# Reordering three places of a two-block network on one core: a sum of squares ahead of a late weight chunk, the convolution between two query chunks, a mixture's first gather under the last gate chunk

## The reference

```python
h = layer_norm(x, ln_in_g, ln_in_b)
for i in range(DEPTH_2):
    proj = h @ w_in[i] + b_in[i]                       # a, g (convolution), q, k, v
    conv_out = conformer_conv(a, g, conv_w[i], conv_b[i], conv_ln_g[i], conv_ln_b[i])
    attn_out = neighbourhood_attention(q, k, v, rpb[i])
    mix = jnp.concatenate([conv_out, attn_out], -1) @ w_out[i] + b_out[i]
    h = layer_norm(DEEPNORM_ALPHA * h + mix, ln1_g[i], ln1_b[i])
    f = swiglu(h, ...) if i % 2 == 0 else moe_swiglu(h, ...)   # 8 experts, top 2, width 3584
    e = jax.nn.sigmoid(h @ ple_gate_w[i] + ple_gate_b[i]) * (p[i] @ ple_w[i])
    h = layer_norm(DEEPNORM_ALPHA * h + f + e, ln2_g[i], ln2_b[i])
```

## Time and profile before

| | |
|---|---|
| median of 3 runs | 2154.37 us (2154.33 to 2155.86) |
| the profiled execution | 2156.51 us, its span 2154.8 us |
| PE busy | 2082.8 us, 97% |
| DVE, ACT, POOL busy | 1569.8, 1282.1, 151.7 us |
| PE's longest waits by line | L969 for DVE 12.4, L613 for the arena-to-arena transfers 10.3 in two |
| share of the chain that ended last | PE 83%, DVE 8%, issue 3%, ACT 2%, DMA 2% |
| HBM | 267 GB/s over the span |

### The profile page before, as it was taken

One profiled execution on the slowest core, in us unless ns is written; L12 is line 12 of the kernel. 1 busy time (PEld: TensorE's weight loads), 2 busy tenths in 40 slices (PEclk: granted clock), 3 DMA queues, 4 the chain that ended last, 5 costly groups with the idle time before them and its releaser, 6 DMA issues.

```text
span 2154.8 us, 29826 instructions
## 1 busy us (share of the span) xinstructions
PE 2082.8 (97%) x11243; PEld 1731.1 (80%) x11243; DVE 1569.8 (73%) x1365; ACT 1282.1 (59%) x1280; POOL 151.7 (7%) x125
## 2 busy tenths in 40 slices
PE   9999999997999999989899999999999999999997
PEld 8977897776788999877677888888888888888875
DVE  6866544576367556646888888888888888888897
ACT  6765443353364334443667777676777777686674
POOL 0041010001024000020130000000000000000100
PEclk9999999999999999999899999999999999999999
DMA  5532594224626555643699999999999999999994
GB/s 217 194 108 99 192 340 163 76 103 169 227 94 224 179 193 179 234 129 123 241 375 392 377 367 379 375 373 369 378 368 368 377 366 378 375 373 368 381 387 183
DMA packets 88530, 581.50 MB, mean 270 GB/s; under 512 B 9968, under 2 KB 14064, under 8 KB 22528
## 3 DMA queue, kind: packets, MB, share of 16 engines
q1 hardware_dynamic: 80336, 549.42, 67.7%
q0 software_dynamic: 7648, 29.89, 3.9%
q10 hardware_dynamic: 464, 1.04, 0.1%
HBM read 559.93 MB, written 15.73 MB: 267 GB/s over the span
## 4 chain that ended last, share of the span: by engine, by line
PE 83%; DVE 8%; issue 3%; ACT 2%; DMA 2%; SPq 1%; POOL 0%; DVEq 0%; POOLq 0%; ACTq 0%
PE bank L613 75%; DVE wrest L2550 3%; DVE wrest L1952 1%; PE bank L1342 1%; SPq L400 1%; DMA ring<-in_w_moe 1%; PE bank L926 1%; PE bank L818 1%; PE bank L1149 1%; PE bank L924 0%; PE bank L905 0%; DMA arena<-arena 0%; DVE bst L2266 0%; DVE h L2276 0%; DVE arena L2524 0%
## 5 line engine op out<-in xcount | busy, mean ns | idle before, releaser
L2550 DVE TENSOR_TENSOR wrest<-ring,whi 128x2048 fp32r<-128x2048 f32 x378 | 853.4, 2307 | 89.8 <-ACT whi L1860 89.5
L1860 ACT ACTIVATE whi<-ring 128x2048 fp32r<-128x2048 f32 x374 | 696.7, 1917 | 70.6 <-DMA ring<-in_w_moe 66.2
L613 PE MATMUL bank<-whi,xgT 128*128 128x512 f32 x1008 | 406.5, 403 | 8.4 <-DVE wrest L2550 6.0
L613 PE MATMUL bank<-wrest,xgT 128*128 128x512 f32 x1008 | 398.0, 395 | 0.0
L613 PE MATMUL bank<-whi,xgR 128*128 128x512 f32 x1008 | 395.1, 392 | 0.0
L613 PEld LDWEIGHTS bank<-whi,xgT 128*128 128x128 f32 x1008 | 190.6, 189 | 53.2 <-DVE wrest L2550 9.6
L613 PEld LDWEIGHTS bank<-whi,xgR 128*128 128x128 f32 x1008 | 190.5, 189 | 46.9
L613 PEld LDWEIGHTS bank<-wrest,xgT 128*128 128x128 f32 x1008 | 189.8, 188 | 39.2
L613 PE MATMUL bank<-whi,hidE 128*128 128x512 f32 x504 | 201.9, 401 | 4.7 <-DVE hidR L2555 4.0
L613 PE MATMUL bank<-wrest,hidE 128*128 128x512 f32 x504 | 198.1, 393 | 0.0
L613 PE MATMUL bank<-whi,hidR 128*128 128x512 f32 x504 | 196.7, 390 | 0.0
(11 more groups left out here) (469 smaller groups left out, 3774.7 us busy)
## 6 DMA issues: line engine op xcount, KB each, us to landing
ring<-in_w_moe SPq DMA_DIRECT2D x378, 1024.0 KB, 4.8
ring<-in_w_dense SPq DMA_DIRECT2D x135, 1024.0 KB, 4.8
row<-in_rows POOLq DMA_DIRECT2D x17, 512.0 KB, 5.5
xg_rows<-ncR POOLq DMA_DIRECT2D x12, 512.0 KB, 24.4
y_rows<-arena POOLq DMA_DIRECT2D x9, 512.0 KB, 6.5
arena<-xg_rows SPq DMA_DIRECT2D x9, 512.0 KB, 5.4
arena<-arena SPq DMA_DIRECT2D x32, 142.0 KB, 5.1
arena<-in_tbias POOLq DMA_DIRECT2D x2, 1536.0 KB, 9.8
```

The lines of the kernel that those rows point to most:

```text
L613: ins = pe.matmul(out_, lhsT, rhs, start=start, stop=stop, **more)
L1860: S["w_hi"].on(a.activation(whi[:, n % HI_SLOTS, :], ring[:, c % RING, :], ACT.Copy))
L2550: S["w_lo"].on(v.tensor_tensor(wrest[:, s, :], ring[:, s, :], whi[:, n % HI_SLOTS, :].bitcast(F32), ALU.subtract))
```

## The change

**Start of layer 0.** ScalarE squares tile 0 of the output product ahead of the rounding of projection chunk 2. VectorE takes the rests of the turned tokens ahead of that chunk's rest.

**Convolution.** The two chunks of the convolution's weights move one place back in the stream of weights, between the two query chunks (`CONV_AT` 9 to 10), so that f 12 and 13 come ahead of the convolution, in both layers. The mean stands between f 14 and f 15. ScalarE copies f 12 and 13 out, and rounds mix chunks 1 and 2, ahead of the convolution's result; mix chunk 0, whose rounded copy lies where `stk` was, comes third. VectorE follows in that order.

**Start of the mixture.** `rank` stands in the middle of gate chunk 2, and `gather_first` behind that chunk, ahead of gate chunk 3. On ScalarE and VectorE the first expert chunks' roundings and rests, the first tokens' split and the gate embedding, now by token tile, are spread over the router's steps. `prime` (counts that stand for a "round minus one" of the loop) comes ahead of them. The transposes of the place matrix, and the copy of their result, move behind the eighth list, to bank 5.

```diff
@@
 PROJ_CHUNKS, MIX_CHUNKS, GATE_CHUNKS, ROW_CHUNKS = 11, 4, 4, 4
-LAYER_CHUNKS, CONV_AT, MIX_AT, GATE_AT = 21, 9, 13, 17
+LAYER_CHUNKS, CONV_AT, MIX_AT, GATE_AT = 21, 10, 13, 17
 SHIFTS, TAP_STEPS = 4, 8
@@
     _names("proj", 0) + _names("pT", 0) + _names("proj", 1, 2) + early + _names("proj", 4, 5, 6, 7, 8, 9, 10)
-    + _names("mix", 0, 1, 2, 3) + _names("gate", 0, 1) + _names("h", 4, 5) + _names("gate", 2, 3) + _names("h", 6, 7)
+    + _names("mix", 1, 2, 0, 3) + _names("gate", 0, 1) + _names("h", 4, 5) + _names("gate", 2, 3) + _names("h", 6, 7)
     for early in (_names("h", 0, 1) + _names("proj", 3) + _names("h", 2, 3),
                   _names("proj", 3) + _names("h", 0, 1, 2, 3)))
-LO_ORDER = (_names("pT", 0) + _names("proj", *range(PROJ_CHUNKS)) + _names("mix", *range(MIX_CHUNKS))
+LO_ORDER = (_names("pT", 0) + _names("proj", *range(PROJ_CHUNKS)) + _names("mix", 1, 2, 0, 3)
             + _names("gate", *range(GATE_CHUNKS)))
@@
                 for i in range(2):
-                    if c == LAYER_FIRST[i] + CONV_AT + 3:
+                    if c == LAYER_FIRST[i] + CONV_AT + 2:
                         stack(i)
@@
 
-                def features(first, end):
+                def features(first, end, between=None):
                     for f in range(first, end):
@@
                             give(1)
+                        elif between:
+                            between()
 
-                features(0, 12)
+                features(0, 14)
                 pe.wait_ge(stk_in, 16 * 16 * (i + 1))
@@
                         give(1)
-                features(12, 14)
-                wait(pe, "conv_ready", 4 * (i + 1))
-                for f in range(4):
-                    mean = pe.matmul(ps[6][:, 0:SEQ], ones, cc[:, f, :], start=f == 0, stop=f == 3)
-                S["cv_ps"].on(mean)
-                features(14, 16)
+
+                def conv_mean():
+
+                    wait(pe, "conv_ready", 4 * (i + 1))
+                    for f in range(4):
+                        mean = pe.matmul(ps[6][:, 0:SEQ], ones, cc[:, f, :], start=f == 0, stop=f == 3)
+                    S["cv_ps"].on(mean)
+
+                features(14, 16, conv_mean)
                 wait(pe, "p_act", 12 * (i + 1))
@@
                 for c in range(ROW_CHUNKS):
-                    ins = half_rows(w[c], c, 1, *hT, half_banks[1])
+                    if i and c == 2:
+                        half_rows(w[c], c, 1, *hT, half_banks[1], (0,))
+                        rank()
+                        half_rows(w[c], c, 1, *hT, half_banks[1], (1,))
+                        gather_first()
+                    else:
+                        ins = half_rows(w[c], c, 1, *hT, half_banks[1])
                     if c == ROW_CHUNKS - 1:
@@
                         turn_logits()
-                    if i and c == 2:
-                        rank()
-                if i:
-                    gather_first()
 
@@
 
-            wait(pe, "places", 3)
-            wait(pe, "m_xgv", 2)
-            for t in range(2):
-                ins = pe.transpose(ps[3][:, t * P:(t + 1) * P], selg[:, t, :], ident)
-            S["place_ps"].on(ins)
             prime(pe, "m_w2", "m_tr")
@@
                 expert_list(i, False)
+            wait(pe, "places", 3)
+            wait(pe, "pg_in", 8)
+            for t in range(2):
+                ins = pe.transpose(ps[5][:, t * P:(t + 1) * P], selg[:, t, :], ident)
+            S["place_ps"].on(ins)
             expert_list(last_list, True)
@@
             copy_m(3)
-            round_proj(0, 2, WO_FIRST)
 
@@
                     square_post(0)
+                    round_proj(0, 2, WO_FIRST)
                     copy_h(0, 0)
@@
 
-                for m in range(6):
+                for m in range(7):
                     if m < 3:
@@
                         round_proj(i, 10, first + 7)
+                        wait(a, "p_dve", 4 * i + 4)
                     for f in (2 * m, 2 * m + 1):
@@
                             keys(f)
+                round_early(1, 9)
+                round_early(2, 10)
                 for f in range(4):
@@
                 round_early(0, CONV_AT + 2)
-                round_early(1, 9)
-                wait(a, "p_dve", 4 * i + 4)
-                keys(12)
-                keys(13)
-                round_early(2, CONV_AT + 3)
                 wait(a, "cn_done", 3 * i + 1)
@@
                         round_dense(FF_FIRST + m, fhi[:, m % FF_HI_SLOTS, :], 0, FF_FIRST - 2 + 2 * m)
-                    gate_embedding(0)
+                    gate_embedding(0, 0)
+                    gate_embedding(0, 1)
 
-            def gate_embedding(i):
+            def gate_embedding(i, j):
 
-                for q in range(4):
-                    j, n = divmod(q, 2)
+                for n in range(2):
                     c = slice(n * 512, (n + 1) * 512)
-                    wait(a, "pg_in", 4 * i + q + 1)
+                    wait(a, "pg_in", 4 * i + 2 * j + n + 1)
                     S["ple_act"].on(a.activation(fe[:, j, c], fe[:, j, c], ACT.Sigmoid))
@@
             layer(1)
-            wait(a, "r_top", 2)
-            S["r_e"].on(a.activation(g12[:, 1, :], g12[:, 0, :], ACT.Exp))
 
@@
             prime(a, "m_sl", "m_hT")
+            round_ahead(0)
+            round_ahead(1)
+            wait(a, "r_top", 2)
+            S["r_e"].on(a.activation(g12[:, 1, :], g12[:, 0, :], ACT.Exp))
+            round_ahead(2)
+            gate_embedding(1, 0)
+            round_gathered(0, 2)
+            round_ahead(3)
+            gate_embedding(1, 1)
             wait(a, "router_done", 1)
             last_list = a.value_load(plan_i[0:1, 1 + SECONDS:2 + SECONDS], min_val=N_EXP - 1, max_val=LISTS - 1)
-            round_gathered(0, 2)
-            for n in range(AHEAD):
-                round_ahead(n)
-            gate_embedding(1)
             def expert_list(i, last):
@@
             def between_post():
-                rest_proj(0, 2)
                 rest_tokens(0, 0)
+                rest_proj(0, 2)
 
@@
                 rest_proj(i, 10)
-                rest_early(0)
                 rest_early(1)
+                rest_early(2)
+                rest_early(0)
 
@@
                                                        ALU.mult, ALU.add))
-                rest_early(2)
                 v.wait_ge(tb_in, 16 * (i + 1))
@@
 
-                    bias_embedding(0)
+                    bias_embedding(0, 0)
+                    bias_embedding(0, 1)
 
-            def bias_embedding(i):
+            def bias_embedding(i, j):
 
                 pb = row_of("ple_b", i + 2)
-                for q in range(4):
-                    j, n = divmod(q, 2)
+                for n in range(2):
                     c = slice(n * 512, (n + 1) * 512)
@@
                     S["pg_in"].on(v.tensor_tensor(fe[:, j, c], ps[half_banks[j][n]][:, :], pb[:, c], ALU.add))
-                v.wait_ge(S["pg_in"].sem, 4 * (i + 1))
-                rows_used.on(v.memset(nmax[:, 3:4], 0.0))
+                if j:
+                    v.wait_ge(S["pg_in"].sem, 4 * (i + 1))
+                    rows_used.on(v.memset(nmax[:, 3:4], 0.0))
 
@@
 
+            def rest_chunk(i, n):
+
+                wait(v, "w_hi", i * E_CHUNKS + (MOE_ROUNDED + n + 1))
+                s = (N_DENSE + n) % RING
+                S["w_lo"].on(v.tensor_tensor(wrest[:, s, :], ring[:, s, :], whi[:, n % HI_SLOTS, :].bitcast(F32),
+                                             ALU.subtract))
+
+            prime(v, "m_hid", "m_hr")
+            rest_chunk(0, 0)
+            bias_embedding(1, 0)
             wait(v, "rl_ps", 1)
@@
             io8 = many(iota[:, 0:N_EXP], 2, 1)
+            rest_chunk(0, 1)
             wait(v, "rl_ps", 2)
@@
 
-            def rest_chunk(i, n):
-
-                wait(v, "w_hi", i * E_CHUNKS + (MOE_ROUNDED + n + 1))
-                s = (N_DENSE + n) % RING
-                S["w_lo"].on(v.tensor_tensor(wrest[:, s, :], ring[:, s, :], whi[:, n % HI_SLOTS, :].bitcast(F32),
-                                             ALU.subtract))
-
             def rest_hid(i, j):
@@
                                                 float(N_EXP - 1), None, ALU.min))
+            rest_chunk(0, 2)
+            rest_gathered(0, 2)
             wait(v, "r_e", 1)
@@
             S["places"].on(v.memset(limit[:, 1:2], 0.0))
-
+            bias_embedding(1, 1)
+            rest_chunk(0, 3)
 
@@
 
-            rest_gathered(0, 2)
-            for n in range(AHEAD):
-                rest_chunk(0, n)
-            wait(v, "place_ps", 2)
-            S["places"].on(v.tensor_copy(selT[:, :, :], ps[3][:, 0:2 * P].rearrange("p (j n) -> p j n", j=2)))
-            bias_embedding(1)
-            prime(v, "m_hid", "m_hr")
             def expert_list(i, last):
@@
                     rest_chunk(i, n)
+                    if last and n == AHEAD + 2:
+                        wait(v, "place_ps", 2)
```

(8 more changed lines are left out.)

## The result

The changed kernel takes **2118.73 us** (median of 4 runs, 2117.69 to 2120.41) against 2155.11 us before (4 runs, 2154.33 to 2156.62): ratio **0.9831**, 95% interval 0.9814 to 0.9848. I had predicted 2117, in a range of 2111 to 2129. The profiled execution took 2120.41 us with a span of 2118.7; the trace of before has 2154.8, so 36.1 us are to be found.

A forecast was written before the change was run, and what follows sets the result against it. TensorE, busy 97% of the span, was taken as the bound, with gains where it stands still or runs slowly. Terms 11.2 + 7.0 + 6.6 + 13.0 = 37.8 us off the 2154.37 median give 2116.6, stated as 2117, range 2111 to 2129.

The forecast's parts named there:

- Part 1: Start of layer 0: squares ahead of the late chunk's rounding bring the second transposes from 522.36 to 511.1, gaining 11.2 us.
- Part 2: Convolution between the query chunks fills the wait for shifted copies: gains 7.0 us in layer 0, 6.6 in layer 1.
- The wait for the query copies: Before the scores, behind the last query tile: TensorE waits 2 us instead of 1.04.
- Rival D: Convolution: shifted copies come later, TensorE stops again, cold; part 2 keeps about 3 of 13.6: 2128; chance 0.08.
- Part 3: Start of the mixture: step 1's transposes of the first list start at 1045.9 instead of 1058.90, gaining 13.0 us.
- a stall of 2.0 us stays, too short, I judge, to cost clock: Before chunk 5 of the first list: TensorE waits 2.0 us beside GpSimd's product, with no loss of clock.
- three places where I wanted a granted clock of 1.00: Sign of being right: full granted clock at layer 0's token transposes, the convolutions and the first expert chunks.
- ScalarE's table loads: Ahead of chunk 5's rest: 7.4 us including two loads of 1.28, with no room for the skill's drain.
- Rival B: First list: five more GpSimd steps by chunk 21 cost 2.1 us each, 10.5 more: 2128; chance 0.08.
- Rival C: First list: expert chunks' transfers set the pace, so part 3 is worth only 5.8 us: 2124; chance 0.08.
- E: Slower: TensorE's clock falls to 1.2 GHz and stays there in the first list; a whole list gives 2234; chance 0.02.
- F: Nothing moves, because what is waited for is not what is named: 2154; chance 0.02.

The follow-up runs named there:

- p2_only: The kernel before with only the convolution moved between the query chunks, squares and mixture as before: 2142.29 us, ratio 0.9938.
- p1_only: The kernel before with only the squares ahead of the late chunk's rounding and VectorE's rests in matching order: 2142.53 us, ratio 0.9939.
- product_second: The changed kernel with GpSimd's first product released by ScalarE's rounding of chunk 5 instead of the start of chunk 4: 2117.72 us, ratio 0.9819.

## Why the prediction was right, and the step that was not

- **Part 1** (11.2 forecast): 10.8 in the trace, 11.0 by its own kernel and when counted from ScalarE's copy. The wait of TensorE is 1.60, where I had 1.5; the clock stayed at 1.00, as judged.
- **Part 2** (7.0 and 6.6): 7.0 and 6.5. The copies into stk come in time for the later convolution. The wait for the query copies is 1.51 where I had 2. Rival D, stops for the shifted copies, is out: 0.34 us in layer 1.
- **Part 3** (13.0): 11.3. The first expert product started at 1002.58, against 1027.2 less the 24.3 that the earlier parts gave, 1002.9. The stop before chunk 5 is 2.25, where I had 2.0. Both are right, the second with some luck: less the same 24.3, VectorE's rest was to start at 1014.4 and take 4.42; it started 0.5 later and took 3.92. **The step that failed is "a stall of 2.0 us stays, too short, I judge, to cost clock".** It cost the clock: chunk 5's products took 1023.32 - 1018.87 = 4.45 us where two chunks take 5.56, so 1.7 us, 1.6 of it by the clock (2.88 behind the stop of 0.63). The part fell short by 1.7; that the stop was 0.2 longer costs nothing more, since TensorE came to it that much earlier. So the six chunks took 20.7 us and not 18.7, and of the three places where I wanted a granted clock of 1.00 only two have it. I had put the term at nothing by judgement, with no row that priced it. It isn't a certain loss either, as p2_only shows: of the 11 stops of 1.91 to 2.33 us in these profiles, 10 have a low clock behind them. The trace of before had told of the low clock, had I asked for it in slices. These are stretches of the kernel before, behind its stops of 2.33 and 2.24 us:

```profile
1044.00:1046.00 2.00, 2.00 (x6) 1.51 (x6) 0.00 (x0) 1.99 (x2) 0.00 (x0) 0.50 0.90 246
...
1056.00:1058.00 2.00, 2.00 (x7) 1.58 (x6) 2.00 (x2) 0.00 (x0) 0.00 (x0) 0.60 0.62 172
1058.00:1060.00 2.00, 2.00 (x8) 1.63 (x7) 1.84 (x1) 0.60 (x2) 0.00 (x0) 0.54 0.84 352
```

I had only the mean of 0.82 over the 27 us around them, and put it down to the first of its stops.
- ScalarE's table loads: from the first load to the start of chunk 5's rest 7.44 us (1007.45 to 1014.89), against 7.4 forecast from the row. The roundings behind these loads start 0.01 us after them. So the drain that the Trainium skill, "ScalarE: Activation LUTs", What ACT_TABLE_LOAD costs, adds to a load isn't seen here.
- Rival B (GpSimd's five other steps cost 2.1 each): the stops beside them are 0.50 and 0.42, as before the change. Rival C (transfers set the pace): the list's row is unchanged, and part 3 gave twice the 5.8 it would have had. E: the clock was low for 4 us, not for a list. F: the waits were what they were named.

The sum came to 36.1 of 37.8. The parts fell short by 0.4, 0.1 and 1.7; the 0.5 behind the turn, which I had not forecast, made up for the first two. That the shortfall of the whole equals that of part 3 is chance.

## What to carry to other kernels

Cost a stop of TensorE by its length and by the clock behind it: here a stop of 1.6 us cost 1.6 and one of 1.9 cost 3.6, while one of 1.84, in the same code, cost its length in nine profiles and some 1.6 us more in five. Where two engines read SBUF by two tiles at once, ask which starts first: moving one wait on GpSimd took 1.6 us from VectorE's critical operation, and so 3.3 from TensorE at that chunk; the next rests took half of it back, and 1.7 was left. A step that has no deadline belongs where the engine that it hinders stands idle, and a burst of small transfers away from the place where the most is due.

## What the runs showed of the hardware

- From 280 us on, the granted clock stayed at 1.00 behind every stop of 1.50 to 1.74 us (1.69 or 1.70 in all 14 profiles, 1.74 in p1_only) but one, which stood right behind a stop of 3.83 (p2_only). Behind the stop of 1.84 or 1.85 at 206 it fell in 5 of 14. Behind stops of 1.91, 2.19, 2.24, 2.25 (six times) and 2.33 it fell to the 1.2 GHz level for 3 to 4 us, with TensorE busy, and came back by itself; behind another stop of 2.24 (p2_only) it stayed at 1.00. In the first 20 us, 2.5 to 3 us behind a stop of 1.3 to 1.7, it fell in three profiles. So between 1.7 and 2.3 us the length of a stop doesn't settle it.
- VectorE's rest (two inputs in SBUF) and GpSimd's two-input product exclude each other, by order of start, even at a distance of 0.14 us. In product_second VectorE's operation with one input in PSUM (L2546 at 1014.97, 0.68 us) kept its time while GpSimd's product went on. GpSimd's scaling step with one input hardly touched VectorE: in the kernel after it ran from 1029.79 to 1033.58, and the four rests from 1031.44 on took 9.13 us, 0.15 more than twice the 4.49 of two. It took 3.2 to 4.2 us itself.
- GpSimd's product started 0.14 us behind VectorE's rest on one event of ScalarE's (product_second). In the kernel after it started 0.57 us behind the start of the TensorE product that released it (1013.68), and 0.17 behind its end.
- Behind GpSimd's four scatters, ScalarE waited 1.4 to 2.5 us at a time for weight chunks, in the kernels before and after, for some 20 us.
